# A second mixer's step list rewritten: convolution chunks among the projections, memory projections among the attention units

## The reference, cut to what matters

```python
n = rms_norm(h, mix_norm[l])
p = n @ w_in[l]
u_conv, q, k, v, q_mem = jnp.split(p, splits, axis=-1)
y_conv = conv_module(u_conv, ...)          # a * sigmoid(gate), 31 causal taps per channel, layer norm, silu
q = apply_rope(rms_norm(q), cos, sin)      # 6 heads of 64
k = apply_rope(rms_norm(k), cos, sin)      # 2 heads
y_swa = sliding_window_attention(q, k, v, swa_sinks[l])
mkv = rms_norm(mem, mem_norm[l]) @ w_mem_kv[l]
mk, mv = jnp.split(mkv, 2, axis=-1)
y_mem = memory_attention(rms_norm(q_mem), rms_norm(mk), mv)
h = h + jnp.concatenate([y_conv, y_swa, y_mem], axis=-1) @ w_out[l]
```

## Time and profile before

| | us |
|---|---|
| time, median of 3 runs | 2863.53 (2862.39 to 2867.09) |
| the profiled execution, first to last instruction | 2863.1 |
| first mixer of this kind, from its first norm to the end of its last sum | 1804.3 to 1993.6, 189.3 |
| the second one | 2440.1 to 2628.6, 188.5 |
| PE busy over the whole span | 2552.3 (89%) |
| DVE, ACT, POOL busy over the whole span | 1380.4, 896.7, 604.7 |

### The profile page before, as it was taken

The page is one execution under the profiler, slowest core; times in us unless marked ns, Lnnn a source line. Parts: engine busy times, 40 slices in busy tenths (PEclk is TensorE's granted clock), DMA queues, the critical chain, the costliest instruction groups (busy, mean ns, idle before and its releaser), DMA issues. The chain is left out here.

```text
span 2863.1 us, 39992 instructions
## 1 busy us (share of the span) xinstructions
PE 2552.3 (89%) x15182; PEld 2150.9 (75%) x15182; DVE 1380.4 (48%) x2486; ACT 896.7 (31%) x1495; POOL 604.7 (21%) x359
## 2 busy tenths in 40 slices
PE   8999998898996999988999699867998699868997
PEld 2227677787995767777898699745998699646996
DVE  7803572425884456142788443274433433374432
ACT  1003334304342333330443333222433333223432
POOL 0000000013331000011333333340331333431331
PEclk9999999998998999999999799978999899968998
DMA  8744233143443333224342454212441555202540
GB/s 310 254 180 179 104 111 111 66 150 135 157 153 116 110 111 109 90 88 155 135 174 88 180 187 185 103 45 88 176 176 44 201 187 186 103 23 91 195 176 37
DMA packets 37260, 391.31 MB, mean 137 GB/s; under 512 B 4384, under 2 KB 5024, under 8 KB 5408
## 3 DMA queue, kind: packets, MB, share of 16 engines
q1 hardware_dynamic: 37152, 389.92, 37.3%
HBM read 388.85 MB, written 1.05 MB: 136 GB/s over the span
## 5 line engine op out<-in xcount | busy, mean ns | idle before, releaser
L667 POOL TENSOR_TENSOR ffn_w_lo<-ring,ffn_w_hi 128x1024 fp32r<-128x1024 f32 x132 | 406.7, 3081 | 728.1 <-ACT ffn_w_hi L632 728.1
L1050 PE MATMUL bank<-h,ring 128*128 128x256 f32 x2048 | 473.8, 388 | 35.9 <-ACT h L959 30.9
L1050 PEld LDWEIGHTS bank<-h,ring 128*128 128x128 f32 x2048 | 392.9, 194 | 112.7 <-issue 40.0
L583 PE MATMUL bank<-ffn_h_hi,ffn_w_hi 128*128 128x256 f32 x2112 | 316.1, 291 | 84.6 <-ACT ffn_h_hi L767 84.6
L583 PEld LDWEIGHTS bank<-ffn_h_hi,ffn_w_hi 128*128 128x128 f32 x2112 | 282.8, 196 | 95.2 <-issue 80.9
L594 PE MATMUL bank<-ffn_g_hi,ffn_w_hi 128*128 128x256 f32 x1056 | 303.5, 287 | 25.7 <-DVE ffn_g_lo L706 25.7
L661 DVE TENSOR_TENSOR ffn_w_lo<-ring,ffn_w_hi 128x2048 fp32r<-128x2048 f32 x126 | 288.9, 2292 | 71.2 <-ACT ffn_w_hi L620 71.2
L583 PE MATMUL bank<-ffn_h_lo,ffn_w_hi 128*128 128x256 f32 x2112 | 303.7, 287 | 0.3
L594 PE MATMUL bank<-ffn_g_lo,ffn_w_hi 128*128 128x256 f32 x1056 | 300.5, 285 | 0.0
L594 PE MATMUL bank<-ffn_g_hi,ffn_w_lo 128*128 128x256 f32 x1056 | 300.4, 284 | 0.0
L583 PE MATMUL bank<-ffn_h_hi,ffn_w_lo 128*128 128x256 f32 x2112 | 300.2, 285 | 0.0
(11 more groups left out here) (250 smaller groups left out, 2981.1 us busy)
## 6 DMA issues: line engine op xcount, KB each, us to landing
ring<-s_in SPq DMA_DIRECT2D x212, 1536.0 KB, 6.3
ring<-ada_in SPq DMA_DIRECT2D x32, 1536.0 KB, 6.6
work<-mem_in SPq DMA_DIRECT2D x2, 1024.0 KB, 4.9
x<-x_in SPq DMA_DIRECT2D x1, 1024.0 KB, 6.2
y_out<-x SPq DMA_DIRECT2D x1, 1024.0 KB, 3.9
con<-con_in SPq DMA_DIRECT2D x1, 801.0 KB, 4.7
par<-par_in SPq DMA_DIRECT2D x2, 302.0 KB, 3.6
work<-pos_in SPq DMA_DIRECT2D x2, 128.0 KB, 3.5
```

The source lines that it names most:

```text
L583: m = pe.matmul(up[j % 2][:, half * T:half * T + T], w_[:, j % 2, c0:c0 + P], (h_lo if part else h_hi)[:, k, :], start=n == 0 and k == 0, ...
L667: pool.tensor_tensor(w_lo[:, j % 2, DOWN], ring[:, (base + j) % RING, DOWN], w_hi[:, j % 2, DOWN], ALU.subtract).then_inc(S(tag + "_down_l ...
L1050: m = pe.matmul(ps[0:m_rows, 0:T], tile(t0 + k)[:, 0:m_rows], rhs, start=k == 0, stop=k == len(src) - 1 and kind != "uk")
```

## The change: what it does

Three things are changed, all in this mixer.

1. The projections ahead of the attention: ca and cg now alternate, and mk (two tiles) and qm (one tile) no longer stand there. Eleven are left of fourteen. The memory's norm, a step `mem` of its own, moves from ahead of the list to the place behind the projection of k.
2. The convolution's chunks 0 to 5, which stood behind the last projection and in units 0 to 5, move among the projections: chunk 0 behind the last cg, chunk 1 behind k and the memory's norm, chunks 2 to 5 each behind one of q, q, q and v. Chunks 6 to 8 move from units 6 to 8 into units 0 to 2.
3. The attention units take the projections mk, mk, qm, qm, mv, mv, one in each of units 0 to 5 (before: qm, mv, mv in units 0, 2 and 4), with the norm of mk in units 1 and 2, that of qm in 3 and 4, and the transposes of mv in unit 6 (before 5).

The first chunk now waits for two gated tiles in place of three. Below, the first lines are a helper that puts extra steps behind the n-th projection; of the list two lines of the new one stand.

```diff
+def after_each(steps, more):
+
+    out, n = [], 0
+    for s in steps:
+        if s[0] == "proj":
+            out += more.get(n, []) if n else []
+            n += 1
+        out.append(s)
+    return out + more.get(n, [])
...
+                     {6: conv(0), 7: [("mem", "", 0)] + conv(1), 8: conv(2), 9: conv(3), 10: conv(4), 11: conv(5)})
...
+              proj("mk", 0) + conv(6), proj("mk", 1) + [("sq", "mk", 0)] + conv(7),
+              proj("qm", 0) + [("sum", "mk", 0), ("rs", "mk", 0)] + conv(8), proj("qm", 1) + [("sq", "qm", 0)],
+              proj("mv", 0) + [("sum", "qm", 0), ("rs", "qm", 0)], proj("mv", 1), [("vt", "mv", 0), ("vt", "mv", 1)],
...
                 def _(pe):
-                    norm_pe(pe, "mm", bank[2], memh)
                     for step, kind, j in STEPS2:
-                        if step == "proj":
+                        if step == "mem":
+                            norm_pe(pe, "mm", bank[2], memh)
+                        elif step == "proj":
...
-                    act.wait_ge(S("mem_in"), 16)
-                    norm_act(act, a, "mm", bank[2], mem, memh, rs_m)
                     for step, kind, j in STEPS2:
-                        if step == "proj" and kind != "out":
+                        if step == "mem":
+                            act.wait_ge(S("mem_in"), 16)
+                            norm_act(act, a, "mm", bank[2], mem, memh, rs_m)
+                        elif step == "proj" and kind != "out":
...
                     norm_dve(dve, v, "mx", sum_bank, x, lambda j: p2("mix_norm", j), h, "_h")
-                    norm_dve(dve, v, "mm", bank[2], mem, lambda j: p2("mem_norm", j), memh, "_h", memh, rs_m)
                     for step, kind, j in STEPS2:
-                        if step == "rs":
+                        if step == "mem":
+                            norm_dve(dve, v, "mm", bank[2], mem, lambda j: p2("mem_norm", j), memh, "_h", memh, rs_m)
+                        elif step == "rs":
...
-                                dve.wait_ge(S("glu_ready"), 3)
+                                dve.wait_ge(S("glu_ready"), 2)
```

More of the change, by code:

```diff
@@ L136, in conv @@
     return [("conv", "", n)]
[L139 to L142, removed]
+def after_each(steps, more):
[6 more added lines that the diff above has]
+    return out + more.get(n, [])
+STEPS2 = (after_each(spread(proj("ca", 0) + proj("cg", 0) + proj("ca", 1) + proj("cg", 1) + proj("ca", 2) + proj("cg", 2)
+                            + proj("k", 0) + proj("q", 2, 0, 1) + proj("v", 0),
+                            [(("qb", 0), ("q", 2)), (("qa", 0), ("q", 1))], [(("qb", 0), ("", 1)), (("qa", 0), ("", 0))], 2),
+                     {6: conv(0), 7: [("mem", "", 0)] + conv(1), 8: conv(2), 9: conv(3), 10: conv(4), 11: conv(5)})
+          + [("vt", "v", 0), ("vt", "v", 1)]
           + attention(10, [
-              proj("qm", 1) + [("sq", "qm", 0)] + conv(1), conv(2), proj("mv", 0) + [("sum", "qm", 0), ("rs", "qm", 0)],
-              conv(3), proj("mv", 1) + conv(4), [("vt", "mv", 0), ("vt", "mv", 1)] + conv(5), conv(6), conv(7), conv(8),
-              [("ln", "", 0)], [("ln", "", 1)], [("ln", "", 2)]])
+              proj("mk", 0) + conv(6), proj("mk", 1) + [("sq", "mk", 0)] + conv(7),
+              proj("qm", 0) + [("sum", "mk", 0), ("rs", "mk", 0)] + conv(8), proj("qm", 1) + [("sq", "qm", 0)],
+              proj("mv", 0) + [("sum", "qm", 0), ("rs", "qm", 0)], proj("mv", 1), [("vt", "mv", 0), ("vt", "mv", 1)],
+              [], [], [("ln", "", 0)], [("ln", "", 1)], [("ln", "", 2)]])
           + proj("out", *range(8)))
```

## The result

| kernel | median us | lowest to highest | runs | profiled span |
|---|---|---|---|---|
| before | 2862.73 | 2860.09 to 2867.09 | 8 | 2863.1 |
| after | 2871.6 | 2865.3 to 2875.8 | 8 | 2870.9 |

The ratio is 1.0028, with a 95% interval of 1.0017 to 1.0038: the change makes the kernel 5 to 11 us slower. The forecast was 2871.7.

The account below looks back on a forecast made before the run. PE bounds the stage ahead of the first scores, and a loop between PE and DVE the attention units. First scores 4.1 us late and units net 0, over two mixers 8.2 us on 2863.5, give 2871.7 us, range 2859 to 2882.

Parts of the forecast that it names:

- Scores of unit 0: Stage ahead of attention: DVE, idle behind the memory's norm and then loaded with chunks, starts the first scores 4 us late.
- The units: Attention units: intervals between DVE's score starts sum to 67.8 against 67.1 us; a 0.7 clock gain cancels the 0.7.
- The sum: Whole kernel: 4.1 us a mixer, twice, 8.2 us on top of 2863.5.
- Terms cancel: Rival: the units' higher clock gives back 2 to 6 us of the 4 us lateness; 2863.5 us, chance 0.26.
- The units win: Rival: matmuls of six units run at the full clock from unit 2 on, -4.3 us a mixer; 2855, chance 0.13.
- The late end: Rival: first scores 7 us late, units 3 us dearer if unit 2 to 3 takes over 12; 2883, chance 0.12.
- Full blocking: Rival: each of 40 taps in chunks 1 to 5 waits for a GpSimd instruction, 24 us a mixer; 2911, chance 0.02.

Follow-up runs that it names:

- e1: The changed kernel with the memory's norm back at the mixer's start, ahead of all projections; 2858.0 us, ratio 0.9983 to before.
- e4: The changed kernel with DVE alone taking its part of the memory's norm behind chunks 1 and 2; 2857.6 us, ratio 0.9979 to before.
- e6: The changed kernel without GpSimd's taps 1 to 30 of the convolution's third tile; 2847.9 us, ratio 0.9944 to before.
- e7: The kernel before without GpSimd's taps 1 to 30 of the convolution's third tile; 2848.4 us, ratio 0.9942 to before.
- e5: e1 with chunks 1 and 2 ahead of the first norm, 3 behind v, 4 to 8 in units 1, 3, 6, 7, 8; 2838.2 us, ratio 0.9910 to before.
- e8: The kernel before with chunks 0 to 2 ahead of the first norm, 3 to 8 in units 1, 3, 4, 6, 7, 8; 2850.2 us, ratio 0.9953.

## Why the prediction was right

The time is right to 0.1 us, which is partly luck: two terms were off by 1.0 and 1.6 us a mixer, in opposite directions. The 0.4 us that I put between span and median is the distance between two different executions; in each of the eight runs of after, the time lies 1.8 or 1.9 us above that run's own span. Nothing in the forecast hangs on it, since its base was the median.

**Scores of unit 0.** Forecast 4.1 us late, measured 5.1 and 5.1. Step by step, in the first mixer of after:

| step, us | predicted | measured |
|---|---|---|
| PE's wait ahead of its first projection | 4.8 | 4.85 |
| PE's wait ahead of the memory's norm | 1.2 | 0.99 |
| DVE idle ahead of that norm | 12.7 | 13.30 |
| the memory's norm on DVE, beside GpSimd (1842.33 to 1848.78) | 6.5 | 6.45 |
| chunks 1 and 2, start to start | 9.4 | 10.25 |
| first norm apply (1859.03 to 1862.49), and the second | 4.3 each | 3.46, about 4 |
| chunk 3, chunk 4 | 4.7 each | 5.24, 5.23 |
| first rotation (1867.73 to 1870.34) | 3.1 | 2.6 |
| DVE's wait at the second rotation | 1.5 | 2.17 |
| chunk 5 | 4.7 | 4.76 |
| PE's waits at the two rotations | about 10 each | 10.07, 10.18 |

The term that was mis-sized is the chunk. I had taken the one chunk that ran beside GpSimd in the units as the price; why it and chunk 5 were cheaper than the others is not shown. Five chunks were 2.0 us dearer (25.5 for 23.5), two norms and two rotations 1.9 us cheaper, the memory's norm began 0.4 us later, and the last wait was 0.7 longer: 1.1 or so in all. My bounds for this term add up to 0 to 8 us late, wider than the 2 to 7 that I wrote. e1 and e4 show that the wait is the cause that decides, and e4 that it acts through DVE's queue: the forecast's reading of "chunk 1 queued behind the waiting instruction" is shown. e6 shows that the price of the chunks comes from GpSimd.

The Trainium skill (SBUF — State Buffer, "Who interferes with whom") says that the later of two instructions at the shared port blocks fully. The trace does not agree: a tap costs 0.64 us beside GpSimd and 0.40 without it, 0.24 more, where the GpSimd instructions beside it are 0.72 and 1.09 long. As a price for each tap the rule overstates by a factor of three to four and a half. In the 10.25 us of chunks 1 and 2 GpSimd was busy for 9.83, and the sixteen taps need 6.40 without it: the two ran at the same time for much of the stretch. That the engines do obstruct each other, e6 and e7 confirm.

**The units.** Forecast 0 net, measured -1.8 and -1.45. The sum hides larger misses. The first two intervals were near (4.8 and 5.1 for 4.70 and 5.50), the third 10.5 for 9.95. The fourth and the sixth were 1.4 and 2.0 shorter than the forecast of 7.2 each, the fifth 1.4 longer than its 10.0. In the short ones it is the clock: in units 0 to 5 it stood at 0.92, where before had 0.71 in 1882.90 to 1929.00. The fourth interval shows it alone. From the release by DVE's probabilities to the end of the next scores PE has the same eleven matmul records in both kernels. They took 3.96 us at a granted clock of 0.50 in before (1908.80 to 1912.76) and 2.96 us at 0.70 in after (1912.27 to 1915.23), DVE waits for them in both, and the interval is 1.0 us shorter. PE's rows of before:

```profile
1908.80 0.90 PE L1588 MATMUL bank<-con,work 128*128 128x128 f32 x3 [5.18 <-DVE work L1810]
...
1911.11 1.65 PE L1578 MATMUL bank<-work 64*128 64x128 f32 x4
```

PE's rows of after:

```profile
1892.39 3.72 PE L1550 MATMUL bank<-work,ring 128*128 128x256 f32 x16
...
1912.27 0.55 PE L1602 MATMUL bank<-con,work 128*128 128x128 f32 x3 [3.92 <-DVE work L1826]
...
1913.58 1.65 PE L1592 MATMUL bank<-work 64*128 64x128 f32 x4
1915.16 6.23 PE L1550 MATMUL bank<-work,ring 128*128 128x256 f32 x16
```

Four of the six projections take 3.72 us, at the full clock. The other two take 5.30 (at 1886.31, behind the wait at the second rotation) and 6.23, and the latter is in the interval of 11.4: PE waits 3.9 us for DVE's normalised probabilities, the granted clock is 0.70 in the products behind that wait and 0.58 in the projection, and the norm of qm waits 5.7 us for the slow projection and for ACT (the L555 row at 1923.66). Chunk 8 has a part in that wait: on DVE it stands between the norm of mk and the scores of unit 3 (1907.11, 2.49 us). In e5, which has no chunk there, PE waits 2.04 us at the same place, the projection takes 3.72 and the interval is 8.05 (9.69 in the second mixer). My condition for this term's failure was a clock above 0.85 in the units. Over all nine intervals it is 0.79, since the last three stand at 0.54; over the six with projections it is 0.92, so there the term failed by my own sign. Against before, the first interval gains most, 2.3 us: six taps of 2.47 us in all stand in it (from 1891.68, when GpSimd has just finished), in place of eight of 4.79 us beside GpSimd. The chunks that left the last three units gave nothing: e5, which has them there, has the same intervals.

**The sum.** First out projection 3.1 and 3.5 us later, 6.65 in all, for the 8.2 of the sum. The spans differ by 7.8: the rest, 1.1, lies outside the mixers, which the change does not touch, where the first mixer of after starts 1.4 us later in its profiled execution. The medians differ by 8.9. So the size of the sum was met roughly (6.65 for 8.2), and the last tenths are chance: what lies outside the mixers made up 1.1, and the base of 2863.5 was 0.8 above the median of the eight runs of before.

**The rivals.** *Terms cancel*: wrong, the units gave back 1.6 of 5.1 us a mixer. *The units win*: the clock did rise as it says, but the fourth and sixth intervals won 3.4 us on the forecast, the fifth lost 1.4 of it, and the scores of unit 0 were 1.0 later. *The late end*: unit 0 was 5.1 late, not 7, and the interval on which it hung was 9.95, not over 12. *Full blocking* would have been 2911.

**What stays open.** e5 and e8 gained 5 and 3 us more than I had allowed at the nearest end. Their intervals show the places, but no run takes their edits one by one. The alternation of ca and cg was never run by itself either. Nor was anything tried that fills DVE's last 9.5 us of idle time.

## What to carry to other kernels

A step that waits stands in the queue of every engine that takes part in it, and blocks there whatever is behind it: ask of each engine apart what is ready and queued behind the wait. In e4 the order of one engine was changed and 14 us came back, with the same work and the same order on the others. Filling work is free only where its engine would otherwise wait: the chunks were free in the last units and cost up to 5.2 us each ahead of the attention, where DVE had become the engine that everyone waits for.

## What the runs showed of the hardware

- A tap on DVE (scalar_tensor_tensor, 128x256, fp32, SBUF) takes 0.40 us start to start alone, and from 0.60 (4.76 for eight in chunk 5) to 0.65 (5.24 for eight in chunk 3) beside GpSimd's taps. GpSimd is slowed as well: its multiply (TENSOR_SCALAR, L1730) takes 0.92 us while DVE is idle and 1.09 beside DVE's taps, its add 0.72 in both, and its 31 taps take 57.2 us in after (1834.51 to 1891.73) and 55.3 in before (1837.35 to 1892.65).
- A projection of sixteen matmul records takes 3.62 to 3.72 us at the full clock and, in after, up to 6.23 behind a wait of PE. In the last units, where only the products of attention run, the granted clock is 0.54 in after and 0.50 in before (1929.00 to 1949.90), close to the lower level of 1.2 GHz, although PE is busy for 14.8 of 22.6 us.
